# Moving 46 fetched expert rows from the value stage into the selection stage, with row numbers written per head

## What is computed

```
q = (xn @ wq) in 8 heads of two halves;  s = q . subkeys (128 keys each half)
v1, i1 = top 16 of half 1;  v2, i2 = top 16 of half 2
top 16 of the 256 sums v1 + v2  ->  idx = i1*128 + i2,  gate = softmax
h = xn . u_tab[idx]           (8 heads x 16 experts = 128 rows for each token)
y = sum(gate * gelu(h) * v_tab[idx])
```

## Time and profile before

| | us |
|---|---|
| median of 3 executions | 3712.5 (3712.1 to 3715.87) |
| the profiled execution | 3716.72 |
| its span, first to last instruction | 3714.9 |
| TensorE matmuls busy | 3515.7 (95%) |
| VectorE busy | 2780.4 (75%) |
| ScalarE busy | 1522.7 (41%) |
| GpSimd busy | 1276.7 (34%) |

### The profile page before, as it was taken

One profiled execution on the slowest core, in us unless ns is written; L12 is line 12 of the kernel. 1 busy time (PEld: TensorE's weight loads), 2 busy tenths in 40 slices (PEclk: granted clock), 3 DMA queues, 4 the chain that ended last, 5 costly groups with the idle time before them and its releaser, 6 DMA issues.

```text
span 3714.9 us, 60532 instructions
## 1 busy us (share of the span) xinstructions
PE 3515.7 (95%) x20002; PEld 3316.9 (89%) x20002; DVE 2780.4 (75%) x5764; ACT 1522.7 (41%) x2306; POOL 1276.7 (34%) x1052
## 2 busy tenths in 40 slices
PE   7999999999998999999899899999999989999997
PEld 5877899999998999999778778999999989999996
DVE  6257478898886888888562664888988878888884
ACT  4334333336664333333333433333476633333333
POOL 0000001218774456665000000022277744565640
PEclk9999799999999999999999988999999999999998
DMA  3200144448889999999222002444588899999981
GB/s 131 80 24 1 46 139 147 145 161 291 299 298 354 370 368 375 371 380 359 92 76 80 7 1 68 139 145 148 179 291 301 298 355 383 367 377 371 367 325 61
DMA packets 266273, 814.24 MB, mean 219 GB/s; under 512 B 24816, under 2 KB 106992, under 8 KB 262512
## 3 DMA queue, kind: packets, MB, share of 16 engines
q1 hardware_dynamic: 92592, 339.05, 25.3%
q0 software_dynamic: 73728, 268.47, 19.2%
q10 hardware_dynamic: 99776, 204.50, 15.4%
HBM read 709.16 MB, written 102.76 MB: 219 GB/s over the span
## 4 chain that ended last, share of the span: by engine, by line
PE 63%; DMA 18%; DVE 10%; issue 5%; POOL 3%; ACT 1%; DVEq 1%; SPq 0%; ACTq 0%; POOLq 0%; PEldq 0%
PE bank L385 16%; PE bank L386 16%; PE bank L387 16%; DMA gath<-slabs,rows_of 10%; DMA gath<-u_rows,rows_of 6%; PE bank L1342 5%; POOL gath L537 2%; PE bank L1122 2%; DVE acc L1982 2%; PE bank L408 2%; DVE wlo L382 1%; PE bank L432 1%; DVE act_w L1943 1%; PE bank L1298 1%; PE bank L1225 1%
## 5 line engine op out<-in xcount | busy, mean ns | idle before, releaser
L382 DVE TENSOR_TENSOR wlo<-raw,whi 128x1024 fp32r<-128x1024 f32 x636 | 803.1, 1263 | 410.1 <-ACT whi L375 377.8
L385 PE MATMUL bank<-act_hi,whi 128*128 128x384 f32 (+1 forms) x2944 | 1054.2, 358 | 22.0 <-DVE act_lo L452 13.7
L386 PE MATMUL bank<-act_lo,whi 128*128 128x384 f32 (+1 forms) x2944 | 1040.7, 354 | 0.0
L387 PE MATMUL bank<-act_hi,wlo 128*128 128x384 f32 (+1 forms) x2944 | 1040.3, 353 | 0.0
L375 ACT ACTIVATE whi<-raw 128x1024 fp32r<-128x1024 f32 x636 | 674.9, 1062 | 500.8 <-PE bank L387 460.0
L385 PE MATMUL bank<-w_hi,whi 128*128 128x384 f32 x2048 | 698.6, 341 | 54.9 <-DVE w_lo L1948 54.7
L386 PE MATMUL bank<-w_lo,whi 128*128 128x384 f32 x2048 | 692.9, 338 | 0.0
L387 PE MATMUL bank<-w_hi,wlo 128*128 128x384 f32 x2048 | 692.6, 338 | 0.0
L529 POOL TENSOR_TENSOR onehot<-onehot,cidx 128x800 f32<-128x800 f32 x56 | 124.0, 2244 | 1547.9 <-DVEq L1833 1547.9
L385 PEld LDWEIGHTS bank<-act_hi,whi 128*128 128x128 f32 x2944 | 558.3, 190 | 64.2 <-issue 13.4
L537 POOL DMA_INDIRECT gath<-slabs,rows_of x256 | 489.1, 1910 | 298.8 <-DVE acc L1982 257.5
(11 more groups left out here) (293 smaller groups left out, 3862.8 us busy)
## 6 DMA issues: line engine op xcount, KB each, us to landing
raw<-slabs SPq DMA_DIRECT2D x636, 512.0 KB
hidden_dram<-hst ACTq DMA_DIRECT2D x256, 192.0 KB
gates_dram<-stage ACTq DMA_DIRECT2D x24, 2048.0 KB
h_sb<-hidden_dram ACTq DMA_DIRECT2D x64, 768.0 KB
g_sb<-gates_dram ACTq DMA_DIRECT2D x32, 1536.0 KB
gath<-u_rows,rows_of POOLq DMA_INDIRECT x256
gath<-slabs,rows_of POOLq DMA_INDIRECT x256
res<-x_t SPq DMA_DIRECT2D x1, 2048.0 KB, 9.1
```

The costliest lines, as they stand in the source:

```text
L382: nc.vector.tensor_tensor(wlo[k][:], raw[k][:], whi[k][:].bitcast(F32), ALU.subtract).then_inc(s_slab_lo, 1)
L385: nc.tensor.matmul(out, a_hi, b_hi, start=first, stop=False)
L386: nc.tensor.matmul(out, a_hi, b_lo, start=False, stop=False)
L387: return nc.tensor.matmul(out, a_lo, b_hi, start=False, stop=last)
```

## The change

Of the 128 u rows of a layer, the first 46 are fetched and used in selection. VectorE writes the row numbers of one head at a time in `sum_experts` and raises `rows_early`. GpSimd fetches, and multiplies each row by the tokens' xn (`product`), in the order: picks of a head, then 3, 7, 7, 7, 7, 7, 8 rows for heads 0 to 6 (`SEL_DOTS`). ScalarE sums each product behind the u slab named in `SEL_AT` (p = 21 to 23, then seven slabs in a row of every nine, and at last 71 to 78), by a copy with an accumulator. xn is turned at p = 4 for this, copied to `xn_early`, and to `x_nat` at p = 78; the scores of head 1 move from p = 5 to p = 6. The gate stage does the next 48 dots, the tail 34, and value has none: it adds v rows from its third slab on, six in the first eight and nine in each later one until the 128 are done. The gelu of all dots now stands in ScalarE's first value slab.

The core of the diff:

```
-DOT_TAIL = 32
+DOT_TAIL = 34
 DOT_GATE = N_BATCH
-DOT_V = P - DOT_GATE - DOT_TAIL
-V_STEP = 12
-V_DOTS = DOT_V // V_STEP
-V_ADDS = P // V_STEP
+SEL_DOTS = (3, 7, 7, 7, 7, 7, 8)
+DOT_SEL = sum(SEL_DOTS)
+SEL_AT = [4 + HEAD_P * (hd + 1) + (8 if hd == 0 else 4) + j for hd in range(PH - 1) for j in range(SEL_DOTS[hd])]
+V_STEP = 9
+V_FIRST = 6
...
+                def gather(n):
+
+                    if GR <= n < DOT_SEL + GR:
+                        pool.wait_ge(S["gath_sel"], n - GR + 1)
+                    elif n >= GR:
+                        pool.wait_ge(S["gath_used"], n - GR + 1 - DOT_SEL)
+                    if n < DOT_SEL + GR - 1 and (n == 0 or n % TOPK == 0):
+                        pool.wait_ge(S["rows_early"], n // TOPK + 1)
+                    table = u_rows if n < P else v_rows
+                    nc.gpsimd.indirect_dma_start(
+                        gath[n % GR][:].rearrange("p k c -> p (k c)"), None, table,
+                        bass.IndirectOffsetOnAxis(ap=rows_of[:, n // P, n % P:n % P + 1], axis=0)
+                    ).then_inc(gath_loaded[n % GR], 16)
+
+                def product(n):
+
+                    if n == 0:
+                        pool.wait_ge(S["xnat_copied"], 2)
+                    r = n % GR
+                    pool.wait_ge(gath_loaded[r], layer * (N_GATH * 4) + (n * 4 + (GR - r) * 4))
+                    nc.gpsimd.tensor_tensor(gath[r][:], gath[r][:], xn_early[:], ALU.mult).then_inc(S["sel_prod"], 1)
+
+                done = 0
                 for hd in range(PH - 1):
                     pool.wait_ge(S["places_ready"], hd + 1)
                     for t in range(NT):
                         rows = onehot[:, t * TOPK:(t + 1) * TOPK, :]
                         nc.gpsimd.tensor_tensor(rows, rows, cidx[:, t, :].unsqueeze(1).to_broadcast([P, TOPK, NC]),
                                                 ALU.mult).then_inc(S["picks_ready"], 1)
-
-                def gather(n):
-
-                    if n >= GR:
-                        pool.wait_ge(S["gath_used"], n - GR + 1)
-                    table = u_rows if n < P else v_rows
-                    nc.gpsimd.indirect_dma_start(
-                        gath[n % GR][:].rearrange("p k c -> p (k c)"), None, table,
-                        bass.IndirectOffsetOnAxis(ap=rows_of[:, n // P, n % P:n % P + 1], axis=0)
-                    ).then_inc(gath_loaded[n % GR], 16)
-
+                    if hd == 0:
+                        for n in range(GR - 1):
+                            gather(n)
+                    for n in range(done, done + SEL_DOTS[hd]):
+                        product(n)
+                        gather(n + GR - 1)
+                    done += SEL_DOTS[hd]
...
-                for n in range(GR - 1):
-                    gather(n)
...
-                    gather(b + GR - 1)
-                for n in range(N_BATCH + GR - 1, N_GATH):
+                    gather(DOT_SEL + b + GR - 1)
+                for n in range(DOT_SEL + N_BATCH + GR - 1, N_GATH):
                     gather(n)
...
-                    if p == P_XNAT:
+                    if p == 4:
                         act.wait_ge(S["xnat_ready"], 1)
                         for c in range(2):
-                            nc.scalar.activation(x_nat[:, 4 * c:4 * c + 4, :], heads(4 + c), ACT.Copy
+                            nc.scalar.activation(xn_early[:, 4 * c:4 * c + 4, :], heads(6 + c), ACT.Copy
                                                  ).then_inc(S["xnat_copied"], 1)
+                    if p == P_XNAT:
+                        act.wait_ge(S["xnat_copied"], 2)
+                        nc.scalar.activation(x_nat, xn_early[:], ACT.Copy).then_inc(S["xnat_late"], 1)
+                    if p in SEL_AT:
+                        n = SEL_AT.index(p)
+                        act.wait_ge(S["sel_prod"], n + 1)
+                        nc.scalar.activation(gath[n % GR][:], gath[n % GR][:], ACT.Copy, accum_out=h_early[:, n:n + 1]
+                                             ).then_inc(S["gath_sel"], 1)
...
+                        if isinstance(it, int) and it == 0 and r == 0:
+                            act.wait_ge(S["tok_dots"], 1)
+                            act.wait_ge(S["gath_sel"], DOT_SEL)
+                            nc.scalar.activation(w_tok[:, 0:DOT_SEL], h_early[:], ACT.Gelu).then_inc(S["tok_gelu"], 1)
+                            nc.scalar.activation(w_tok[:, DOT_SEL:P], h_tok[:, DOT_SEL:P], ACT.Gelu
+                                                 ).then_inc(S["tok_gelu"], 1)
...
+                    if p == 4:
                         for k in range(KD):
-                            out = heads(4 + k // 4)[:, k % 4, :]
+                            out = heads(6 + k // 4)[:, k % 4, :]
                             nc.tensor.matmul(out, act_hi[:, k, TD:T].bitcast(F32), ident, start=True, stop=False)
                             last = nc.tensor.matmul(out, act_lo[:, k, TD:T].bitcast(F32), ident, start=False, stop=True)
                         last.then_inc(S["xnat_ready"], 1)
...
+                    if p == 6:
+                        pe.wait_ge(S["xnat_copied"], 2)
+                        scores(1)
+                    if p > 4 and SEQ[p - 1][0] == "q" and SEQ[p - 1][1] % 2 == 1:
+                        scores(SEQ[p - 1][1] // 2)
...
-                pe.wait_ge(S["xnat_copied"], 2)
+                pe.wait_ge(S["score_read"], PH)
...
+                    step(V.tensor_scalar(rows_of[:, 0, hd * TOPK:(hd + 1) * TOPK], expert[:, NTD, hd, :],
+                                         par[:, Q_ROWS:Q_ROWS + 1], None, ALU.add))
+                    settle()
+                    dve.sem_inc(S["rows_early"], 1)
...
-                        dot(q * 8 + b, b % GR)
+                        dot(q * 8 + (DOT_SEL + b), (DOT_SEL + b) % GR)
...
+                def ready_tokens():
+
+                    dve.wait_ge(s_used, S_V)
+                    for i in range(2):
+                        V.memset(acc[i][:], 0.0).then_inc(S["acc_zero"], 1)
+                    dve.wait_ge(S["tok_gelu"], 2)
+                    V.tensor_tensor(w_tok, w_tok, g_tok[:], ALU.mult).then_inc(S["tok_ready"], 1)
+                    dve.wait_ge(S["acc_zero"], 2)
+                    dve.wait_ge(S["tok_ready"], 1)
...
+                            add_row(base + c, (slot + c) % GR)
+                        if isinstance(it, int) and it == 0 and r >= 8 - V_FIRST:
+                            if r == 8 - V_FIRST:
+                                ready_tokens()
+                            add_row(r - (8 - V_FIRST), (r - (8 - V_FIRST)) % GR)
...
+                eight_values(0, 0, 0, False)
+                with dve.Fori(0, 3) as i4:
+                    for o in range(4):
+                        eight_values(i4 * 4 + (1 + o), (1 + o) % 2, i4 * 2 + (1 + o) // 2, False, V_STEP,
+                                     i4 * (4 * V_STEP) + (V_FIRST + o * V_STEP), V_FIRST + o * V_STEP)
+                for it in range(13, NKEYS // 8):
+                    base = V_FIRST + (it - 1) * V_STEP
+                    eight_values(it, it % 2, it // 2, it == NKEYS // 8 - 1, max(0, min(V_STEP, P - base)), base, base)
```

More of the change, by code:

```diff
@@ L87 @@
 REGION = 53200
-assert N_SLABS == S_WG + 8 and DOT_V == 48 and (S_WQ + P_GATE) % RING == 0
+assert N_SLABS == S_WG + 8 and DOT_SEL + DOT_GATE + DOT_TAIL == P and SEL_AT[-1] < P_GATE and (S_WQ + P_GATE) % RING == 0
 C_ID, C_ONE, C_TRI, C_CHUNK, C_NEGT, C_POSD, C_M16, C_M32, C_M64 = [P * i for i in range(9)]
@@ L948, in eight_values @@
                             load_g(it + 2, odd)
-                with act.Fori(0, V_DOTS // 2) as i2:
+                        if isinstance(it, int) and it == 0 and r == 0:
[4 more added lines that the diff above has]
+                                                 ).then_inc(S["tok_gelu"], 1)
+                eight_values(0, 0, False)
+                eight_values(1, 1, False)
+                with act.Fori(1, NKEYS // 16 - 1) as i2:
                     for odd in range(2):
                         eight_values(i2 * 2 + odd, odd, False)
[L952 to L956, removed]
-                for it in range(V_DOTS + V_ADDS, NKEYS // 8):
+                for it in range(NKEYS // 8 - 2, NKEYS // 8):
                     eight_values(it, it % 2, it == NKEYS // 8 - 1, False)
@@ L1953, in _ @@
                     if x < DOT_TAIL // 2:
-                        dot(DOT_GATE + 2 * x, 2 * x % GR)
-                        dot(DOT_GATE + 2 * x + 1, (2 * x + 1) % GR)
+                        for n in (DOT_SEL + DOT_GATE + 2 * x, DOT_SEL + DOT_GATE + 2 * x + 1):
+                            dot(n, n % GR)
                     if x == 2:
@@ L1983, in add_row, with eight_values @@
                                            ALU.add).then_inc(S["gath_used"], 1)
-                def eight_values(it, odd, it2, final, work=(), per=0, base=0):
+                def ready_tokens():
[6 more added lines that the diff above has]
```

(27 more changed lines are left out.)

18 lines of the change are left out of this document (9 added, 9 removed).

## The result

The kernel became slower: the median of eight runs is 3732.28 us, beside 3704.11 for the kernel before in the same session, a ratio of **1.0074** (95% interval 1.0055 to 1.0093). The forecast was 3650, with a range of 3626 to 3700. What happened is the first rival, at a lower price than its worst case. The profiled execution took 3731.39 us, with a span of 3729.6.

A forecast was written before the change was run, and what follows sets the result against it. Value was taken as DMA-bound at 4.59 us a slab, TensorE-bound after. Gain 85.6, less 2 for tail and 21.4 for selection, made 62.2 off 3716.7: 3654.5, or 3650 against the runs' median; range 3626 to 3700.

The forecast's parts named there:

- the first rival: Selection: GpSimd products block VectorE's two-input steps, making VectorE the bound; at worst 3782 us; chance of slower 0.11.
- Selection, what it does to VectorE: Selection heads: each GpSimd row product delays VectorE by 0.8 us, from possible 0 to 2.2; arrears some 7 us.
- the term of 21.4 us for selection: End of selection: TensorE waits 3.7 us for lost cover plus 7 of VectorE's arrears, 10.7 us a layer.
- 50c - 37.6: Selection: VectorE's arrears in us a layer if each GpSimd row product costs VectorE c us.
- The turning point: Selection: cost per product, c = 1.5 us, from which VectorE's arrears decide, 42 us a layer.
- xn turned at p = 4: Selection: TensorE's transposition, moved early, no longer covers VectorE's closing chain; TensorE waits 3.7 us more a layer.
- The end of selection: Before the transposes of sel: TensorE idle about 11 us, from 3.7 of lost cover and 7 of arrears.
- The prediction is wrong if heads are longer: Stated test in selection: heads longer than 41.9 us would mean VectorE had become the bound.
- Value: Value stage: nine rows per eight slabs make TensorE the bound, 4.18 us a slab, gain 85.6 us over both layers.
- Rival 2: Value stays bound by transfers, in bursts bridged by only four row buffers: 4.35 us a slab, 3694 us; chance 0.14.
- Rival 4: Selection: row numbers come too late for early gathers, GpSimd and ScalarE stand still at p = 21; 3680 us, chance 0.02.
- Against it: the splits of rows 8 lost 1.36 and about 0.45 us: Argument against VectorE becoming selection's bound: two VectorE splits traced beside GpSimd's picks products lost less than a whole product.

The follow-up runs named there:

- the first experiment: The changed kernel with GpSimd's 46 row products a layer cut from 1024 to 8 columns, all else kept: 3647.83 us, ratio 0.9849.

## Why the prediction was wrong, point by point

- **Selection, what it does to VectorE: the step that failed.** "I take 0.8 each, 5.6 us for seven" was too low by half, and with it the term of 21.4 us for selection, where 103.0 was measured. It is 1.5 to 1.6 us, by the windows (1.5 in the head shown, 46.1 - 35.2 - 0.45 over seven, and 1.2 to 1.65 in the others; 1.55 over the stage), by the timeline, and by the first experiment: 43 us a layer in the rival's own arrears, 50c - 37.6, give c = 1.6. The turning point had been put at 1.5. Three things stood behind the 0.8. A product was taken to begin at random; in fact GpSimd's stream is products and gather issues back to back (35.5 us of 47), and in the head from 664 us six of nine splits, four by row products and two by picks, and the conversion and one short step besides, are held up. One-input steps were taken as free, since the Max steps are; the conversions are not (3.14 for 0.23 us). And the short two-input steps of the parts between splits weren't counted: each can cost a whole product and the issue ahead of it. The rows of before showed two splits held up per head; with four products in a head, that could not say how often a product hits when there are eleven.
- The Trainium skill, SBUF — State Buffer, section "Who interferes with whom", says that a VectorE instruction with two SBUF inputs contends with a GpSimd one that reads SBUF, not with one that only writes, and that conversions can take the shared ports. The trace agrees on the product (37 splits held), the write (33 of 33 splits free) and the conversions (3.14 us for 0.23). It does not agree that whoever is first holds the way for its whole length where GpSimd reads one tile: there 39 splits run free beside the last 1.6 us of a 2.47 us step.
- **The product's duration**: 2.2 predicted, 2.42 measured. **ScalarE's sum**: 1.25 against 1.05 + 0.19; that the sums lie beside other work is right but for 4.7 and 6.3 us a layer.
- **xn turned at p = 4**: 3.7 us predicted, 3.6 measured. **The end of selection**: TensorE idle 12.7 us before the transposes for about 11 predicted, the stretch 35.0 us for 24.4. Right, but it was only the last of the arrears: three slabs of lead were used up earlier, and the heads grew by 1 to 10 us, where the prediction had them at 41.9. "The prediction is wrong if heads are longer" was the right test.
- **Value**: 4.18 us a slab predicted, 4.23 and 4.22 measured; 75.0 gained for 85.6. TensorE is the bound, the DMA share 0.92. The term was 10.6 us too large: two eights of a stage take some 2 us more, where VectorE's loop turns and it is idle for 3.4 us with no wait that the profile names (why, stays open), and the last takes 37.4 us, as before. Rival 2 fell.
- **The gelu** costs ScalarE a wait of 3.5 us in the first value slab for the 8.19 of the earlier trace rows. **Gate**: nothing, right. **Tail**: a cost of 2 predicted, 2.8 gained, within what such stretches vary. Rival 4, late row numbers, fell: ScalarE never waits for a product.
- **The chances.** "Against it: the splits of rows 8 lost 1.36 and about 0.45 us" priced what four products do in a head with slack; VectorE, at 84% before and asked for seven more, deserved the worse bound. At 2.2 us each the rival had 3782; it came out at 3732, because a product cost 1.6 and not all of its 2.4 us. Two slips of arithmetic bear on nothing: the middle of 4.14 and 4.59 is 4.37, a gain of 38 for 42, and the lower end by its own terms is 3624 for 3626.

## What to carry to other kernels

Work handed to GpSimd is not off VectorE if both read two tiles: price it at what remains of each GpSimd step when a VectorE step begins, for short steps and conversions too. Here that was 1.5 to 1.6 us of a 2.4 us product, more than the 1.2 of VectorE's own dot. A one-input step on GpSimd cost a sixth, and a write held up no two-input step, only a conversion. Look at the products that were there already, too: moved in time, the four of the picks held VectorE up for 33 us a layer instead of 13. Before moving work to a third stage, look at what stands behind a waiting instruction: 24 rows beside gate cost 70 to 76 us a layer when GpSimd's gathers waited for the dot of the same batch, 15 to 21 one batch later, and twelve of them cost gate nothing.

## What was not expected of the hardware

GpSimd products back to back can leave VectorE no turn between them. Timeline of the kernel after: four products of the picks and one of a row stand back to back from 578.20 to 587.44, and one split, begun in the second, lasts through all the others.

```profile
576.92 1.26 POOL L538 DMA_INDIRECT gath<-u_rows,rows_of  x1 [0.69 <-ACT gath L857]
578.20 6.89 POOL L556 TENSOR_TENSOR onehot<-onehot,cidx 128x800 f32<-128x800 f32 x4
585.04 2.40 POOL L549 TENSOR_TENSOR gath<-gath,xn_early 128x1024 f32<-128x1024 f32 x1
...
580.03 8.50 DVE L386 TENSOR_TENSOR wlo<-raw,whi 128x1024 fp32r<-128x1024 f32 x1
```

It takes 8.50 us for 1.23. In the kernel with products of 8 columns one of 8.28 stands at the same place, and one of 8.1 to 8.3 in each of the next four heads, so it isn't the long product that does it; the heads there keep their 41.9 us, so VectorE's slack took it. In the earlier trace rows VectorE got its turn after the first product of the picks, and the second took 2.73. That split began 0.24 us into the first product; the one of 6.51 us in the kernel with VectorE's dots began 1.48 us into it, and got no turn. What decides stays open.
